# Decoder layer on one core: the bit-by-bit search's scratch words in PSUM, and the reciprocals of the row sums spread over 64 columns before they are transposed

## The reference

```python
score = jnp.einsum('bqh,bqhl->bql', w, jax.nn.relu(s))
score = jnp.where((k_pos[None, :] <= q_pos[:, None])[None], score, -jnp.inf)
idx = lax.top_k(score, n_top)[1]                  # n_top = 256
...
probs = jax.nn.softmax(jnp.where(valid, logits + bias, -jnp.inf), axis=-1)
out = jnp.einsum('bqcgk,bqkcd->bqcgd', probs.astype(v_sel.dtype), v_sel)
```

## Time and profile before

| | us |
|---|---|
| median of 3 runs | 1594.22 |
| lowest, highest | 1593.73, 1594.70 |
| the profiled execution, whole | 1596.34 |
| its span, first to last instruction | 1594.6 |

### The profile page before, as it was taken

One profiled execution on the slowest core, in us unless ns is written; L12 is line 12 of the kernel. 1 busy time (PEld: TensorE's weight loads), 2 busy tenths in 40 slices (PEclk: granted clock), 3 DMA queues, 4 the chain that ended last, 5 costly groups with the idle time before them and its releaser, 6 DMA issues.

```text
span 1594.6 us, 25832 instructions
## 1 busy us (share of the span) xinstructions
PE 1531.3 (96%) x9489; PEld 1371.1 (86%) x9489; DVE 963.1 (60%) x2173; ACT 573.9 (36%) x1171; POOL 610.2 (38%) x548
## 2 busy tenths in 40 slices
PE   7998999989998999999999999999999999999997
PEld 6863566656995667999999999999999999999996
DVE  5326989897997775223448755455555454555545
ACT  4324354325214665222335422413224223132233
POOL 4111009275545321111123834626437255263350
PEclk9999999999998999999999999999999999999999
DMA  5431011132110012320012201102102011021002
GB/s 177 106 106 53 21 41 27 31 104 65 53 41 1 2 41 62 96 81 28 27 40 80 80 27 54 54 25 79 53 26 79 26 53 53 26 79 53 26 13 108
DMA packets 91556, 87.60 MB, mean 55 GB/s; under 512 B 17046, under 2 KB 82214, under 8 KB 91469
## 3 DMA queue, kind: packets, MB, share of 16 engines
q1 hardware_dynamic: 83671, 75.45, 15.2%
q0 software_dynamic: 2688, 8.39, 1.7%
q10 hardware_dynamic: 5118, 2.69, 0.6%
HBM read 78.30 MB, written 8.45 MB: 54 GB/s over the span
## 4 chain that ended last, share of the span: by engine, by line
PE 58%; DVE 1%; POOL 1%; issue 1%; ACT 0%; DMA 0%; DVEq 0%; POOLq 0%
PE banks L2028 27%; PE banks L2125 16%; PE banks L108 13%; PE banks L1985 0%; PE banks L1966 0%; PE banks L2142 0%; DVE yo L2602 0%; POOL wL L2176 0%; DMA out_dram<-yo 0%; ACT XH L2244 0%; POOL hnL_lo L2189 0%; DVE hnL_hi L2457 0%; POOL dL L2173 0%; POOL T4L L2189 0%; ACT sH L2237 0%
## 5 line engine op out<-in xcount | busy, mean ns | idle before, releaser
L2176 POOL TENSOR_TENSOR wL<-w_raw,wH 128x512 fp32r<-128x512 f32 x176 | 231.5, 1330 | 314.8 <-ACT wH L2287 313.8
L2028 PE MATMUL banks<-hnH,wH 128*128 128x344 f32 x704 | 225.8, 321 | 2.2 <-POOL wL L2176 0.8
L2028 PE MATMUL banks<-hnH,wL 128*128 128x344 f32 x704 | 224.7, 319 | 0.0
L2589 DVE TENSOR_TENSOR resid<-resid,banks 128x344 f32<-128x344 f32 x264 | 132.1, 512 | 96.7 <-PE banks L2125 96.7
L2125 PE MATMUL banks<-aH,dH 128*128 128x344 f32 x528 | 169.3, 321 | 0.0
L2125 PE MATMUL banks<-aH,dL 128*128 128x344 f32 x528 | 169.1, 320 | 0.0
L2125 PE MATMUL banks<-aL,dH 128*128 128x344 f32 x528 | 168.2, 319 | 0.0
L1480 DVE TENSOR_SCALAR_CACHE_REDUCE pta<-SC,thr 128x384 uint8<-128x384 f32 (+4 forms) x160 | 144.0, 930 | 2.2 <-POOL SC L921 0.2
L2287 ACT ACTIVATE wH<-w_raw 128x512 fp32r<-128x512 f32 x176 | 109.7, 626 | 73.3 <-PE banks L2028 40.5
L2028 PEld LDWEIGHTS banks<-hnH,wH 128*128 128x128 f32 x704 | 132.1, 188 | 3.2 <-issue 1.9
L2028 PEld LDWEIGHTS banks<-hnH,wL 128*128 128x128 f32 x704 | 132.3, 188 | 0.0
(11 more groups left out here) (407 smaller groups left out, 3628.9 us busy)
## 6 DMA issues: line engine op xcount, KB each, us to landing
w_raw<-in_w_gate_up_dram SPq DMA_DIRECT2D x22, 1024.0 KB, 5.0
d_raw<-in_w_down_dram SPq DMA_DIRECT2D x11, 1024.0 KB, 4.8
big<-in_w_in_dram SPq DMA_DIRECT2D x12, 512.0 KB, 3.7
W<-in_x_prompt_dram SPq DMA_DIRECT2D x8, 512.0 KB, 5.5
slab_raw<-in_w_in_dram SPq DMA_DIRECT2D x8, 512.0 KB, 3.8
x_nat<-in_x_prompt_dram SPq DMA_DIRECT2D x8, 512.0 KB, 4.1
slab_raw<-in_w_out_dram SPq DMA_DIRECT2D x8, 512.0 KB, 3.6
out_dram<-yo SPq DMA_DIRECT2D x8, 512.0 KB, 3.5
```

The lines of the kernel that those rows point to most:

```text
L2028: last = mm(out, W_[w][s][:, i * P:(i + 1) * P], x_of(x)(i), start=start and i == 0 and j == 0, stop=stop and i == HALF - 1 and j == 2)
L2176: gp.tensor_tensor(wL[s].rearrange("p (k n) -> p k n", k=HALF), quadrant(x, *HOME[name]), f32(wH[s]).rearrange("p (k n) -> p k n", k=HALF) ...
L2589: V.tensor_tensor(resid[:, m, chunk(DOWN_ORDER[o])], resid[:, m, chunk(DOWN_ORDER[o])], ps[:, 4 + n % 4, 0:CH], ALU.add).then_inc(y_done, 1)
```

## The change

Three things are edited.

1. `update` takes the tile for the rejected bits as an argument. All rounds but the first ones of blocks 2 and 3 (those between the score units) now write them to PSUM, bank 5, columns 480 to 486, and read them from there. `lane_tot` moves to bank 5 too, columns 496 and 497.
2. So that no other engine touches bank 5 meanwhile, the chunks of the three projections go round 5 banks instead of 6, and the small products of the decode tokens move by one bank.
3. `invert_sums` writes each reciprocal 64 times, so the output is 128 x 512 instead of 128 x 8 (in the free tile `late`), and `transpose_sums` becomes four transposes of 128 x 128.

```diff
-                    if x >= 6:
-                        pe.wait_ge(uq_evac, x - 5)
+                    if x >= ROT:
+                        pe.wait_ge(uq_evac, x - ROT + 1)
...
                     for t in range(4):
-                        for f in range(2):
-                            last = mm(ps[f * HD:(f + 1) * HD, slot_bank(sums_slot[i]), t * P:(t + 1) * P], ri[:, 2 * t + f:2 * t + f + 1].to_broadcast([P, HD]),
-                                      ident[:, :], start=True, stop=True, tile_position=(0, f * HD))
+                        last = tr(ps[:, slot_bank(sums_slot[i]), t * P:(t + 1) * P], ri_wide[:, t * P:(t + 1) * P], ident[:, :])
...
+                rej_bank = ps[:, 5, 480:480 + NSEL + 1].bitcast(I32)
+                lane_tot_bank = ps[:, 5, 496:498]
+
+                def update(cols, found, bit, rejected):
+                    stepped(V.tensor_scalar(rejected[:, cols], found, float(TOPK), bit_value(bit), ALU.is_lt, ALU.mult))
...
-                    V.tensor_reduce(lane_tot[:, :], lane_cntT[:, :].rearrange("p (b r) -> p b r", r=16), AX.X, ALU.add).then_inc(lane_step, 1)
+                    V.tensor_reduce(lane_tot_bank, lane_cntT[:, :].rearrange("p (b r) -> p b r", r=16), AX.X, ALU.add).then_inc(lane_step, 1)
...
-                    V.reciprocal(ri[:, :], rs[:, i % 2, :]).then_inc(ri_ready, 1)
+                    V.reciprocal(ri_wide.rearrange("p (h d) -> p h d", h=NH), rs[:, i % 2, :].unsqueeze(2).to_broadcast([P, NH, HD])).then_inc(ri_ready, 1)
```

More of the change, by code:

```diff
@@ L318, in decoder_layer @@
             rs = sb("rs", [P, 2, NH])
-            ri = sb("ri", [P, NH])
+            ri_wide = late[:, 0:512]
             x_in = [sem(f"x_in{b}") for b in range(3)]
@@ L406, in decoder_layer @@
             PROJ = KD * NCH
+            ROT = 5
             K_FROM = 11
@@ L618, in slab_chunk @@
                         pe.wait_ge(big_in[n % 2], 16 * (n // 2 + 1) if n < U_ITEMS else 32 + 32 * ((n - U_ITEMS) // 2 + 1))
-                    if x >= 6:
-                        pe.wait_ge(uq_evac, x - 5)
+                    if x >= ROT:
+                        pe.wait_ge(uq_evac, x - ROT + 1)
                     for k in range(KD):
-                        last = mm(ps[:, x % 6, 0:CH], big[:, n % 2, k, :], hT[:, k, chunk(c)], start=k == 0, stop=k == KD - 1)
+                        last = mm(ps[:, x % ROT, 0:CH], big[:, n % 2, k, :], hT[:, k, chunk(c)], start=k == 0, stop=k == KD - 1)
                     last.then_inc(uq_ready, 1)
@@ L628, in join_sample_heads @@
                         for f in range(2):
-                            mm(ps[:, 5 + f, NB * j:NB * j + NB], kid[f * 32:(f + 1) * 32, 0, j * P:(j + 1) * P], wsel[f * 32:(f + 1) * 32, :],
+                            mm(ps[:, 6 + f, NB * j:NB * j + NB], kid[f * 32:(f + 1) * 32, 0, j * P:(j + 1) * P], wsel[f * 32:(f + 1) * 32, :],
                                start=True, stop=True)
-                    mm(ps[:, 7, 0:1], wselx[:, :], rsn[:, :], start=True, stop=True).then_inc(ssc_ready, 1)
+                    mm(ps[:, 6, P:P + 1], wselx[:, :], rsn[:, :], start=True, stop=True).then_inc(ssc_ready, 1)
                 def transpose_sample_scores():
@@ L771, in _ @@
                         pe.wait_ge(small_in[m % 2], 16 * (m // 2 + 1))
-                    if x >= 6:
-                        pe.wait_ge(p_evac, x - 5)
+                    if x >= ROT:
+                        pe.wait_ge(p_evac, x - ROT + 1)
                     for k in range(4):
-                        last = mm(ps[:, x % 6, 0:CH], small[:, m % 2, k, :], aP[:, k, c * CH:(c + 1) * CH], start=k == 0, stop=k == 3)
+                        last = mm(ps[:, x % ROT, 0:CH], small[:, m % 2, k, :], aP[:, k, c * CH:(c + 1) * CH], start=k == 0, stop=k == 3)
                     last.then_inc(p_ready, 1)
@@ L787, in _ @@
                         x = NCH * m + c
-                        if x < 6:
-                            pe.wait_ge(p_evac, PROJ - 5 + x)
+                        if x < ROT:
+                            pe.wait_ge(p_evac, min(PROJ - 3 + x, PROJ))
                         else:
-                            pe.wait_ge(g_evac, x - 5)
+                            pe.wait_ge(g_evac, x - ROT + 1)
                         for a, k in enumerate(G_ORDER):
@@ L795, in _ @@
                             for j, (w, v) in enumerate((("hi", "hi"), ("hi", "lo"), ("lo", "hi"))):
-                                last = mm(ps[:, x % 6, 0:CH], G_[w][s][:, k * P:(k + 1) * P], X_[v][:, k, chunk(c)],
+                                last = mm(ps[:, x % ROT, 0:CH], G_[w][s][:, k * P:(k + 1) * P], X_[v][:, k, chunk(c)],
                                           start=(a == 0 and j == 0), stop=(a == KD - 1 and j == 2))
@@ L1283, in _ @@
                     act.wait_ge(p_ready, x + 1)
-                    A(M[:, m, chunk(c)], ps[:, x % 6, 0:CH], ACT.Copy).then_inc(p_evac, 1)
+                    A(M[:, m, chunk(c)], ps[:, x % ROT, 0:CH], ACT.Copy).then_inc(p_evac, 1)
                     if 12 <= x < 18:
@@ L1491, in score_unit, with pair_round @@
                         V.scalar_tensor_tensor(scs[i], src, w, scs[i], ALU.mult, ALU.add).then_inc(score_step, 1)
-                def pair_round(cols, blocks, r):
+                def pair_round(cols, blocks, r, rejected):
                     for c, i in enumerate(blocks):
@@ L1497, in pair_round, with early_rounds @@
                     dve.wait_ge(counted, counts[0])
-                    update(cols, cntA[:, 0:2], BITS - 1 - r)
+                    update(cols, cntA[:, 0:2], BITS - 1 - r, rejected)
                 early = [0]
-                def early_rounds(n):
+                def early_rounds(n, rejected):
                     for r in range(early[0], min(early[0] + n, BITS)):
-                        pair_round(slice(3, 5), (2, 3), r)
+                        pair_round(slice(3, 5), (2, 3), r, rejected)
                     early[0] += n
@@ L1511, in _ @@
                     if n >= 2 * IH and n % 3 == 2:
-                        early_rounds(2)
-                early_rounds(EARLY_ROUNDS - early[0])
+                        early_rounds(2, rej)
+                early_rounds(EARLY_ROUNDS - early[0], rej_bank)
                 dve.wait_ge(causal_done, NSEL)
```

35 lines of the change are left out of this document (16 added, 19 removed).

## The result

| | before | after |
|---|---|---|
| median, us (4 runs each) | 1594.31 | 1619.89 |
| lowest, highest | 1593.73, 1594.70 | 1613.88, 1623.60 |
| ratio, 95% interval | | 1.0155 [1.0137, 1.0174] |
| span of the profiled execution | 1594.6 | 1615.6 |

The change costs 25.6 us in the median. The forecast was 1613.5 with a range of 1603 to 1625: right in sign and in its main cause, 6.4 us short in size.

What follows compares the result with a forecast made beforehand. TensorE was taken as the bound except in a hole from 484.1 to 490.3 us. Hole -3.6, reciprocal +18.9, transposes -2.8 and clock +6.8 gave +19.3 us, so 1613.5 us, range 1603 to 1625.

Steps and rivals of the forecast that it cites:

- the hole: From 484.1 to 490.3 us TensorE works only 0.71 us and VectorE 6.09, so a gain for VectorE counts there.
- first 16.5 us: VectorE's saving on tiny operations from 190 to 287 us; brings nothing, since TensorE has 0.12 us idle there.
- The 3.6 us: Gain before the attention: masks ready earlier, so VectorE's first row minimum starts at 485.8 instead of 489.39 us.
- The tiny operations: Writing PSUM, they nearly all stop waiting for GpSimd: 16.5 us less from 190 to 287, 22.6 from 371.6 to 490.
- Five banks at nothing: Projection chunks wait for the emptying five chunks back; ScalarE empties in time, so no cost.
- The wide reciprocal: Attention block ends: 512 columns take 3.29 us and TensorE waits for all of it, eight stalls, loss 18.9 us.
- rival D: Broadcast columns are cheaper, the 512 reciprocals take 0.69 us, and the kernel gets faster, 1588.8 us; chance 0.06.
- Transposes, 2.8 us: Four transposes at the attention's block ends take 0.53 us instead of 0.92 on TensorE's path, gain 2.8 us.
- The clock in the attention, 6.8 us: TensorE's stalls bring two falls to half clock, 3.4 us each; bounds none and five (17 us).
- The way in sum: All terms together: -3.6 + 18.9 - 2.8 + 6.8 = +19.3 us.
- a pause of TensorE before 484 us that wasn't there: Sign that would prove the prediction wrong about the five banks.

Runs made afterwards that it cites:

- run 1: Changed kernel with the narrow reciprocal (128 x 8) and eight matmuls put back, PSUM scratch and five banks kept: 1595.2 us, ratio 0.9986 to the kernel before.
- run 4: Kernel before with only the rotation over five banks and the moved small products, scratch words in SBUF: 1595.1 us, ratio 0.9998 to the kernel before.
- run 5: Changed kernel with five overwritten 128 x 256 matmuls at seven block ends where TensorE waits for the reciprocal: 1616.8 us, ratio 1.0116 to the kernel before.
- run 12: Changed kernel with eight overwritten 128 x 256 matmuls in three TensorE pauses ahead of the decode products with the values: 1614.1 us, ratio 1.0110 to the kernel before.

## Why the prediction was right, and where it fell short

- **What bounds the kernel, and the hole.** Right. VectorE's first 16.5 us bring no gain that shows: the first decode product starts at 376.1 to 385.0 us in the profiles with the scratch words in PSUM and at 380.2 to 386.0 in the others. The masks are early, VectorE waits 25.2 us for its first row minimum, and GpSimd ends last. The 3.6 us were 3.9 by run 1. In the changed profile the row minimum starts at 489.13 and not at 485.8, since the gates end 3.3 us later; from the gates' end it is 2.3 us, as forecast.
- **The tiny operations.** They lose 16 and 22 us as forecast, down to 160 to 190 ns each. The Trainium skill ("SBUF — State Buffer", section "Who interferes with whom") says that a VectorE instruction with at most one SBUF input, outside the two-port modes, does not contend with GpSimd; these rows agree.
- **Five banks at nothing.** Right, by run 4.
- **The wide reciprocal.** Right: 3.34 us for 3.29, stalls of 19.1 for 18.9, the first seven within 0.03 us of their forecasts and the last 0.3 over. The column costs (3343 - 190) / 504 = 6.26 ns, a broadcast input or not. The estimate from the Trainium skill ("VectorE: DVE Perf Modes", section "First, the fixed hardware budget"), 4.4 us, is too high by a third, and rival D is out.
- **Transposes, 2.8 us.** Right at full clock: 0.59 us from L849 to L841 at the end of block 2, and the 16.3 of run 5 against run 1 matches 19.1 - 2.8. At half clock, as at the end of block 1, L849 to L841 is 1.05 us, and the gain is gone there.
- **The clock in the attention, 6.8 us.** Right in kind, a little low: 8.8 (run 5). That the size came out so near is luck. I expected two falls of 6.8 us; it was four of 3.4 us and a longer one at the start, so more falls, each half as long, and stalls of 2.0 us brought some too, where I had a pause of 1.6 without one as my bound.
- **The way in sum:** forecast +19.3, measured +21.2.
- **What the sum left out.** The clock's term looked at the attention alone. That parts 1 and 2 could go with a half clock in the decode tokens' products was in neither the sum nor a rival; "The first 16.5 us bring nothing" stands for that whole part of the kernel. It costs 7.1 us in the trace and 5.8 in the median (run 12, with the spread given there). Without it the changed kernel takes 1614.1, and the forecast was 1613.5. One of the signs of being wrong that the prediction names, "a pause of TensorE before 484 us that wasn't there", did come in the short pauses at 320 to 346 us, though they sum to less than the pauses they replace (5.5 us against 6.8).
- **The noise.** I took 0.2% as what can be told from no change by three runs within 1 us. Over 88 runs the kernel before spreads over 10.7 us, and the slower ones have the lower granted clock (0.981 at 1600.7 us, 0.991 at 1590.2). The range of 1603 to 1625 was made wide for falls in the attention; that it also held the 7.1 us of a place it hadn't thought of is luck. So is how near the traces come, 21.0 us for 19.3: the 7.1 are met there by the 7.3 us that the first and the last part of the kernel happened to be shorter.

## What to carry over

An edit that gives nothing in one part of a kernel can still go with a lower clock there: compare the granted clock of every stretch, not only of the one where the loss is expected. The price of this reciprocal is set by the columns that it computes, so compute the eight reciprocals and spread them by something cheap. If the wide form must stay, pieces behind each pair take the stall away from the engine that waits, though here the kernel's time was still 3.6 us above the kernel before. And where TensorE falls to half clock behind short pauses, try a few matmuls whose result is thrown away: in the means they were worth some 3 to 6 us here, about as much as parts 1 and 2. Judge all of it by many runs: the 12 of one kernel here spread over up to 13 us.

## What was new of the hardware

- In the changed kernel TensorE stays at 0.50 while it is busy for 15.46 of 15.9 us with the decode tokens' products (376 to 391.9 us), and is back at full clock at 395.5 us, 3.6 us into the gate products. In run 12 the same products begin at full clock, take 8.1 us and keep it.
- An added float32 matmul of 128 x 256 is two instructions of TensorE, together 0.43 us from start to start at full clock (run 12); eight of them in pauses of 1.2, 0.6 and 0.5 us went with a full clock in four of four profiles.
- A copy of 128 x 512 from SBUF to SBUF with a broadcast input takes 0.43 us, and up to 1.15 us beside GpSimd. With an operand in PSUM, L1453 and L1455 over 2 and 3 columns take 158 to 166 ns throughout the search.
